# First heads chosen one by one, scores inside the next block, GLA output among the last input blocks, and both ends cut shorter, in a two-layer hybrid trunk

## What is computed

```python
hn = rms_norm(h, mix_norm[0]); h = h + gla_dilated_mixer(hn, ...)      # layer 0
hn = rms_norm(h, ffn_norm[0]); h = h + peer_ffn(hn, ...)
hn = rms_norm(h, mix_norm[1]); h = h + rglru_mixer(hn, ...)            # layer 1
hn = rms_norm(h, ffn_norm[1]); h = h + peer_ffn(hn, ...)
return rms_norm(h, final_norm)

# gla_dilated_mixer: gated linear attention (GLA, 4 heads) beside windowed attention (8 heads)
proj = h @ w_in
o_gla = gla_chunked(gq, gk, gv, log_a)
o_gla = o_gla * rsqrt(mean(o_gla * o_gla) + eps)                       # per head
o_gla = o_gla * head_gain * silu(gg)
return concatenate([o_gla, o_att]) @ w_out

# peer_ffn: 8 heads, 16 of 16,384 experts for each head and row
q = hf @ w_query;  s = q . sub_keys                                    # two halves of 128 keys
top_s, top_i = top_k(s, 16)                                            # of each half
best_s, best_c = top_k(all sums of a first and a second half, 16)      # ids = 128 * first + second
g = softmax(best_s)
out = sum over the 128 chosen of gelu(u[id] . x) * g * v[id]
```

## Time and profile before

| | us |
|---|---|
| median of 3 runs (lowest, highest) | 3009.1 (3007.6, 3010.1) |
| the profiled execution | 3012.2 |
| its span, first to last instruction | 3010.4 |
| busy in it: PE, DVE, ACT, POOL | 2663.3, 2155.2, 636.8, 992.6 |
| DMA over the span | 1,182.34 MB, mean 393 GB/s |

### The profile page before, as it was taken

One profiled execution on the slowest core, in us unless ns is written; L12 is line 12 of the kernel. 1 busy time (PEld: TensorE's weight loads), 2 busy tenths in 40 slices (PEclk: granted clock), 3 DMA queues, 4 the chain that ended last, 5 costly groups with the idle time before them and its releaser, 6 DMA issues.

```text
span 3010.4 us, 34985 instructions
## 1 busy us (share of the span) xinstructions
PE 2663.3 (88%) x11992; PEld 2185.1 (73%) x11992; DVE 2155.2 (72%) x6642; ACT 636.8 (21%) x1693; POOL 992.6 (33%) x1028
## 2 busy tenths in 40 slices
PE   8889999999999888989999898989999788877887
PEld 6778888767887676867887676868787566555555
DVE  1237867888578878677688777778678777678565
ACT  3221211163212216101111215201212110102001
POOL 0003333333323233333333333333333334333332
PEclk9899999999999999999999999999999999999999
DMA  5339999999999999999999999999999999999997
GB/s 181 103 133 421 419 424 409 426 381 402 411 398 387 402 426 414 414 427 426 426 407 419 414 427 418 407 426 424 427 415 392 409 426 424 427 425 411 427 426 330
DMA packets 166642, 1182.34 MB, mean 393 GB/s; under 512 B 19376, under 2 KB 19904, under 8 KB 23872
## 3 DMA queue, kind: packets, MB, share of 16 engines
q0 software_dynamic: 147456, 1073.81, 86.1%
q1 hardware_dynamic: 19008, 106.31, 9.0%
HBM read 1177.95 MB, written 2.10 MB: 392 GB/s over the span
## 4 chain that ended last, share of the span: by engine, by line
PE 52%; DMA 26%; DVE 12%; issue 8%; ACT 1%; POOL 0%; DVEq 0%; SPq 0%; ACTq 0%; POOLq 0%
PE main_bank L318 33%; DMA main_ring<-in_uv,main_idi 26%; PE main_bank L354 10%; PE main_bank L352 5%; DVE main_diagonal L301 2%; DVE main_ring L287 2%; DVE main_pick L199 1%; PE main_bank L522 1%; DVE main_pick L193 1%; DVE main_hid L287 1%; DVE main_topi L162 1%; DVE main_work L154 1%; DVE main_idf L206 1%; DVE main_topi L156 1%; PE main_bank L714 0%
## 5 line engine op out<-in xcount | busy, mean ns | idle before, releaser
L318 PE MATMUL main_bank<-main_ring,main_diagonal 128*128 128x256 f32 (+1 forms) x8160 | 1980.5, 389 | 301.4 <-DVE main_diagonal L301 300.3
L318 PEld LDWEIGHTS main_bank<-main_ring,main_diagonal 128*128 128x128 f32 x8160 | 1529.3, 192 | 660.0 <-DVE main_diagonal L301 440.7
L287 DVE CUSTOM_DVE_ANT_0 main_ring<-main_ring,main_bank 128x1024 f32<-128x1024 f32 x1024 | 1247.6, 1218 | 621.0 <-DMA main_ring<-in_uv,main_idi 609.7
L270 POOL DMA_INDIRECT main_ring<-in_uv,main_idi x1024 | 992.4, 969 | 1994.0 <-PE main_bank L318 1740.1
L292 ACT ACTIVATE main_act_out<-main_hid 128x1 f32<-128x1 f32 x1024 | 206.2, 203 | 2156.1 <-DVE main_hid L287 2154.9
L301 DVE TENSOR_SCALAR main_diagonal<-main_ident,main_act_out,main_gate 128x128 f32<-128x128 f32 x1024 | 358.8, 350 | 23.0 <-ACT main_act_out L292 14.0
L354 PE MATMUL main_bank<-main_xT,main_w_block 128*128 128x256 f32 x1408 | 359.3, 382 | 1.8 <-ACT main_xT L387 1.8
L354 PEld LDWEIGHTS main_bank<-main_xT,main_w_block 128*128 128x128 f32 x1408 | 269.1, 192 | 39.2 <-ACT main_xT L387 2.2
L354 PE MATMUL main_bank<-main_xT_query,main_w_block 128*128 128x256 f32 x512 | 124.9, 381 | 0.9 <-ACT main_xT_query L387 0.9
L354 PEld LDWEIGHTS main_bank<-main_xT_query,main_w_block 128*128 128x128 f32 x512 | 97.3, 191 | 15.1 <-ACT main_xT_query L387 1.2
L292 ACT ACT_TABLE_LOAD x82 | 105.2, 1283 | 1.4
(11 more groups left out here) (187 smaller groups left out, 1209.8 us busy)
## 6 DMA issues: line engine op xcount, KB each, us to landing
main_w_block<-in_w_query SPq DMA_DIRECT2D x32, 1024.0 KB, 9.4
main_w_block<-in_w_ab SPq DMA_DIRECT2D x24, 1024.0 KB, 8.0
main_ring<-in_uv,main_idi POOLq DMA_INDIRECT x1024, 10.7
main_w_block<-in_w_c_in SPq DMA_DIRECT2D x16, 1024.0 KB, 9.3
main_w_block<-in_w_out SPq DMA_DIRECT2D x8, 1024.0 KB, 6.9
main_w_block<-in_w_c_out SPq DMA_DIRECT2D x8, 1024.0 KB, 9.1
main_att_bias<-in_att_bias SPq DMA_DIRECT2D x16, 256.0 KB, 5.2
main_resid<-in_x SPq DMA_DIRECT2D x2, 1024.0 KB, 7.5
```

Of the source, the lines that this page charges most:

```text
L270: nc.gpsimd.indirect_dma_start(self.ring[n % self.bufs], None, self.uv[p // NT], bass.IndirectOffsetOnAxis(self.choice.idi[:, p % 2, k:k + ...
L287: self.nc.vector.tensor_tensor_reduce(out=row, in0=row, in1=self.ps[:, 6:8], scale=1.0, scalar=0.0, op0=ALU.mult, op1=ALU.add, accum_out=s ...
L318: last = self.nc.tensor.matmul(self.ps[:, 4 + at // T, at % T:at % T + wide], self.diagonal[:, n % DIAGS], self.ring[n % self.bufs][:, D + ...
```

## The change

1. Start: x is loaded as two tiles with a semaphore each, and the squares of a tile wait for it alone; ident and gains are waited for later. A Sqrt of a constant stands first on ScalarE.
2. GLA, first half: the two output tiles follow input pieces 169 and 174 (PE), 172 and 178 (ACT). The sigmoid of the gate goes in two halves of 256 columns, the first after piece 186, and now waits for GLA's squares, since its tile is moved onto theirs. The scale and head gain are applied to the output ahead of the gate, the gate in two halves. The turn of the mixed rows does the attention half first and waits for GLA in between. The second half of the rows uses the same functions in the ring, at k = 86 to 94.
3. Query: scores of head i-1 stand after the fourth piece of block i. ScalarE's exponential comes after all four query copies.
4. Choice: heads 0 and 1 are ranked and chosen one at a time; a semaphore `first` releases the first 16 gathers. Head 2's ranking moves into the ring at k = 5.
5. End: the last add, squares, scaling and store go in two halves of 512 columns; a Sqrt of a constant stands before the last squares.

```diff
-    def candidates(self, dve, g):
+    def candidates(self, dve, g, ks=range(2)):
...
+        nc, n, of = self.nc, len(ks), slice(ks[0], ks[-1] + 1)
...
-        nc.vector.tensor_copy(self.idi[:, p % 2, slots], self.idf[:]).then_inc(self.chosen, 1)
+        copied = nc.vector.tensor_copy(self.idi[:, p % 2, slots], self.idf[:, ks[0] * PK:(ks[-1] + 1) * PK])
+        if ks[-1] == 0:
+            copied.then_inc(self.first, 1)
+            return
+        copied.then_inc(self.chosen, 1)
...
-                if k % (2 * PK) == 0:
+                if n == 0:
+                    pool.wait_ge(self.choice.first, 1)
+                elif n == PK or k % (2 * PK) == 0:
                     pool.wait_ge(self.choice.chosen, p * self.choice.PAIRS + k // (2 * PK) + 1)
...
+    def add_halves(self, dve):
+
+        dve.wait_ge(self.half_done, 1)
+        for a in range(2):
+            if a:
+                dve.wait_ge(self.v_done, 2 * NT * HK)
+            half = self.resid[:, NT - 1, a * T:(a + 1) * T]
+            self.nc.vector.tensor_tensor(half, self.ps[:, 4 + a], half, ALU.add).then_inc(self.half_added, 1)
...
-        self.sg = own("gla_sg", 1024, [P, 2, GV_W])
+        self.sg = own("gla_sg", 2048, [P, 2, GV_W])
...
-        pe.wait_ge(self.gla_done, g + 1)
-        for d in range(KD):
+        for d in (4, 5, 6, 7, 0, 1, 2, 3):
+            if d == 0:
+                pe.wait_ge(self.gla_done, g + 1)
...
-    def gla_silu_act(self, act, g):
-        act.wait_ge(self.dec_there, g + 1)
-        act.wait_ge(self.w.taken, self.until(g, 11))
-        self.nc.scalar.activation(self.sg[g][:], self.gg[:], ACT.Sigmoid).then_inc(self.silu, 1)
+    def gla_silu_act(self, act, g, c):
+
+        act.wait_ge(self.ssd, g + 1)
+        act.wait_ge(self.w.taken, self.until(g, 10 + c))
+        cols = slice(c * BC, (c + 1) * BC)
+        self.nc.scalar.activation(self.sg[g][:, :, cols], self.gg[:, :, cols], ACT.Sigmoid).then_inc(self.silu, 1)
...
+    def gla_gated_dve(self, dve, g, c):
+
+        dve.wait_ge(self.silu, 2 * g + c + 1)
+        cols = slice(c * BC, (c + 1) * BC)
+        o, sg = self.mixed[g][:, :, cols], self.sg[g][:, :, cols]
+        self.link(dve, self.nc.vector.tensor_tensor(sg, sg, self.gg[:, :, cols], ALU.mult))
+        last = self.nc.vector.tensor_tensor(o, o, sg, ALU.mult)
+        if c:
+            last.then_inc(self.gla_done, 1)
...
+    def sqrt_act(self, act):
+
+        act.wait_ge(self.one_there, 1)
+        self.nc.scalar.activation(self.one[:, 1:2], self.one[:, 0:1], ACT.Sqrt)
...
-            sp.dma_start(resid[:, 0:2], x[:, 0:2]).then_inc(loaded[0], 16)
+            for t in range(2):
+                sp.dma_start(resid[:, t], x[:, t]).then_inc(x_in[t], 16)
...
-            act.wait_ge(loaded[0], 48)
+            final.sqrt_act(act)
             for t in range(2):
+                act.wait_ge(x_in[t], 16)
                 norms.squares(act, 0, mix0.rows[0], t)
             norms.root_mean(act, 0)
             norms.rows_scaled(act, 0, mix0.rows[0])
+            act.wait_ge(loaded[0], 32)
...
+                if n in (172, 178):
+                    mix0.gla_out_act(act, 0, n // 178)
+                if n == 186:
+                    mix0.gla_root_act(act, 0)
+                    mix0.gla_silu_act(act, 0, 0)
...
                 tail0.act_q(act, 0, i)
-                if i:
-                    tail0.act_scores(act, 0, i - 1)
-                if i == 2:
-                    choice.exponentials(act, 0, 0)
+                if i < 3:
+                    tail0.act_scores(act, 0, i)
+            choice.exponentials(act, 0, 0)
             norms.gains_in(act, 2, mix0.xT)
...
-            final.squares_act(act, NT - 1)
+            final.sqrt_act(act)
+            final.last_squares_act(act)
             final.root_act(act, NT - 1)
...
-            for i in range(3):
+            for i in range(2):
                 tail0.rank_dve(dve, 0, i)
-                if i == 1:
-                    choice.candidates(dve, 0)
-                    choice.greatest(dve, 0)
-                    choice.places(dve)
-                    choice.picked(dve)
-                    choice.numbers(dve, 0, 0)
+                choice.candidates(dve, 0, (i,))
+                choice.greatest(dve, 0, (i,))
+                choice.places(dve, (i,))
+                choice.picked(dve, (i,))
+                choice.numbers(dve, 0, 0, (i,))
...
-                        if k in (9, 17, 25, 33, 41):
+                        if k in (5, 9, 17, 25, 33, 41):
                             tail0.rank_dve(dve, 0, k // 8 + 2)
...
-            for t in range(2):
-                mix0.gla_out_pe(pe, 0, t)
+                if n in (169, 174):
+                    mix0.gla_out_pe(pe, 0, n // 174)
...
-            for i in range(4):
-                tail0.pe_query(pe, 0, i)
+            for x in range(4 * weights.PIECES):
+                tail0.pe_query_piece(pe, 0, x, 3)
```

More of the change, by code:

```diff
@@ L136, in __init__ @@
         self.links = 0
[L137 to L138 removed]
+        self.chain, self.diff, self.exped, self.first, self.chosen, self.gated = (
+            s.sem(f"choice_{x}") for x in ("chain", "diff", "exped", "first", "chosen", "gated"))
     def link(self, dve, ins):
@@ L319, in sum_rows @@
                                          self.ring[n % self.bufs][:, D + at:D + at + wide], start=k == 0, stop=k == HK - 1 and at % T + wide == T)
+            if n == 2 * NT * HK - 1 and at + wide == T:
+                last.then_inc(self.half_done, 1)
         last.then_inc(self.v_done, 1)
@@ new lines, in start_dve, with last_squares_act @@
+    def start_dve(self, dve):
+        self.nc.vector.memset(self.one[:, 0:1], 1.0).then_inc(self.one_there, 1)
+    def sqrt_act(self, act):
+        act.wait_ge(self.one_there, 1)
+        self.nc.scalar.activation(self.one[:, 1:2], self.one[:, 0:1], ACT.Sqrt)
+    def last_squares_act(self, act):
+        for a in range(2):
+            act.wait_ge(self.experts.half_added, a + 1)
+            cols = slice(a * T, (a + 1) * T)
+            self.nc.scalar.activation(self.rows[:, NT - 1, cols], self.resid[:, NT - 1, cols], ACT.Square, scale=float(D) ** -0.5,
+                                      accum_out=self.halves[:, a:a + 1]).then_inc(self.squared, 1)
@@ new lines, in last_mean_dve, with last_dve @@
+    def last_mean_dve(self, dve):
+        dve.wait_ge(self.squared, NT + 1)
+        self.nc.vector.scalar_tensor_tensor(self.ms[:, NT - 1:NT], self.halves[:, 0:1], EPS, self.halves[:, 1:2], ALU.add,
+                                            ALU.add).then_inc(self.mean, 1)
+    def last_dve(self, dve):
+        nc, c = self.nc, NT - 1
+        dve.wait_ge(self.rooted, NT)
+        nc.vector.reciprocal(self.rs[:, c:c + 1], self.root[:, c:c + 1]).then_inc(self.scaled, 1)
+        dve.wait_ge(self.scaled, NT)
+        for a in range(2):
+            cols = slice(a * T, (a + 1) * T)
+            nc.vector.scalar_tensor_tensor(self.rows[:, c, cols], self.resid[:, c, cols], self.rs[:, c:c + 1], self.gain[:, cols], ALU.mult,
+                                           ALU.mult).then_inc(self.there, 1)
```

102 lines of the change are left out of this document (49 added, 53 removed).

## The result

Median **2991.9 us** (2989.3 to 2992.9, 4 runs) against 3009.6 for the kernel before beside it (3007.6 to 3014.2, 4 runs): ratio 0.9938, 95% interval [0.992, 0.9955]. The interval leaves out 1, so the kernel is faster, by 17.7 us in this pair, where 25.5 was forecast; 2991.9 lies 1.4 us above the range. In four later sessions the changed kernel came out as here and the kernel before slower: over all sessions the kernel before takes 3014.2 us in the mean (84 runs), the changed kernel 2991.3 (19 runs). That is a gain of **22.9 us**.

A forecast was written before the change was run, and what follows sets the result against it. PE paces the input blocks, then PE and DMA the gathers; gains lie outside that ring. Start 2.6, GLA output 8.7, clock 2.1, first sum 9.6 and end 2.5 sum to 25.5: 3009.1 to 2983.6 us, range 2978.5 to about 2990.5.

The forecast's parts named there:

- the ring: Gathers of expert rows through 7 buffers, from PE's first expert sum: some 2,770 us that the change hardly enters.
- the clock: At the output projection: its first 64 records would no longer start at the lower PE clock, 2.1 us saved, bounds 0 to 2.1.
- Start: Kernel start: x in halves and the Sqrt table loaded early bring the first transpose 2.6 us forward, bounds 1.1 to 3.1.
- GLA output: Between input blocks and output projection: output tiles made among the last input pieces, projection 8.7 us earlier, bounds 6.5 to 9.5.
- first two heads: Query to first expert sum: earlier scores, heads chosen singly, exponential later; first sum 9.6 us earlier, bounds 8 to 11.6.
- end: After the last expert sum: add, squares, scaling and store in halves, Sqrt loaded early; 2.5 us saved, bounds 1.4 to 3.0.
- Does the ring start with PE: PE is full from the first expert sum, so everything after it shifts by 23.0 us; by the gathers' side 24.6.
- rival 1: Gathers carry the shift into later passes: 1.6 us more, 2.0 with a warm first sum; 2980.0 to 2982.0, chance 0.20.
- rival 2: PE's clock falls around GLA's output: 2.1 us lost, up to 3.1 more; 2985.7 to 2988.8 us, chance 0.20.
- The base, and the range: Span differences taken off the 3009.1 us median; range about 2978.5 to 2990.5, with 1.5 us for run differences at the low end.
- My own test for being wrong: Sum wrong if the first expert sum moves 23 us and the last does not, or 2,770 us between them changes by over 2.
- The slower rival (emptier ring): Buffers come back too late for the DMA queues, passes 3.7% longer: 74 us over 1,980 us, 3057 us, chance 0.02.

The follow-up runs named there:

- the fill: Changed kernel plus 14 unused identity transposes in PE's wait for GLA's gate and 4 ahead of the output projection: medians 2987.9 and 2989.4 us.

## Why the prediction was right and wrong

Two steps failed. The sum booked 2.1 us for the clock as a sure gain, and it took the rest of the kernel, base and ring, as known to 1.5 us. The parts that were added up from rows of waits held.

The first sum, in the mean of the profiles of the whole kernels (two before, four after):

```
                                            forecast   measured
start, to the first product                     2.6       2.4
first input block                               0         1.1
second input block to projection (GLA)          8.7       8.4
clock on the projection                         2.1      -0.85
first query block to first sum                  9.6       9.9
together                                       23.0      20.95
```

- **Start (2.6), GLA output (8.7), first two heads (9.6), end (2.5): right.** Measured in the first pair 2.39, 8.9 (149.41 - 138.13 - 2.39, of which 0.2 is the first input block), 9.6 and 2.45. (The start's two terms add up to 2.7, not 2.6; the second square begins 1.3 us earlier, not 1.6.) The added Sqrt load and SP's extra issue cost no more than was said: the first query block begins 169.27 - 138.13 = 31.1 us behind the projection (before 33.3, less the 2.1 of the clock), and the wait ahead of the first sum is the ACT chain alone. What the third head's move costs inside the ring is below what its scatter lets one see. Choosing one head took 9.6 us (180.42 to 190.01), forecast 9.7.
- **"Does the ring start with PE": right.** PE is at 199.12 of 199.80 us from the first sum on, and rival 1, the gathers' side, got nothing: the ring is not shorter.
- **The clock (2.1): this step failed.** I took two numbers of one profile, 16.20 and 14.08, for a price that the place always pays and that the change takes away. What the clock costs the projection is a toss in both kernels: 0.8 us before in the mean of five profiles, 2.2 after in the mean of seven, so the change loses some 1.4 us where I booked 2.1 as won. That the first pair showed the 2.1 us to the digit was luck, one profile of seven. Over the whole-kernel profiles the term was 3.0 us off, and the first input block, booked at nothing, gave 1.1 back (a toss as well, and perhaps partly the new start): 229.6 - 208.7 = 20.9 us, not 23.0. The reading that transposes hold the clock up was right, as the fill shows, though the rise at 225 us that I gave for it came in one profile of four; that waits of 1.9 and 0.9 us (measured 2.02 and 0.74) would not let it fall was wrong. This is rival 2's mechanism, given 0.20, and it should have been the likelier case, since in the profile of before PE had slowed behind a wait of just 0.85 us.
- **The base, and the range: this step failed too, and is the larger part of the miss.** Working in differences of one execution and taking them off a median of three runs (3009.1) was the plan; but the ring of one program varied by 5.5 us between four executions, and the kernel before takes 3014.2 in the mean. I allowed 1.5 us for it, at the low end of the range only, although the four times at hand (3007.6 to 3012.2) were already 4.6 apart. From 2983.6 to 2991.3 are 7.7 us: 5.1 of base, 2.1 of clock and first block, 0.5 of ring and tail, which is within the uncertainty. A range with 3 us of run scatter at both ends (the deviation of single runs is 3.2) would have held it.
- **My own test for being wrong misled.** I had written that a ring changed by over 2 us would refute the sum. It changed by 6.2 in the first pair and by 0.5, give or take 1, in the mean: one pair of profiles can't decide 2 us out of 2,770.
- The slower rival (emptier ring) did not come: 402 and 417 GB/s for 403 and 418.

**Open:** why the ring varies. The extra of the first pair is spread over passes of both signs (differences by 128 steps, in us: -0.6, +2.6, +2.8, -1.7, +2.9, -3.0, +0.4, +2.7). Over the 16 profiles its length goes weakly with the time that the clock spent at the lower level inside it (54.6 to 103.9 us; correlation 0.44, which 16 unrelated pairs reach in about one case of twelve): 60.0 us went with 2771.7 and 88.5 with 2777.8, but 103.9 with 2773.8. No run here separates cause from chance.

## What to carry to other kernels

Ahead of this long ring, which one engine paces at its start, what was taken from the chain to its first step was kept: 22.9 us by the runs, 23.4 by the rows of first sum and tail. The terms that were waits could be added up from rows to a few tenths. A gain that rests on the granted clock is a chance, not a duration: read several profiles, and where PE's waits can't be removed, try to fill them with transposes (here some 2.4 us of 2991). And take as the base of a forecast, and as its uncertainty, what many runs of the kernel show: the part that nothing touches was here the largest source of error.

## What the runs showed of the hardware

In the last 80 steps or so, where gathers pace the ring at one dot product per 2.4 us, every 32nd gather lands 1.0 us late, three times, in both kernels and at the same spacing (steps 952, 984, 1016 before; 944, 976, 1008 after). DVE's timeline of the changed kernel, the second row 3.42 us after the first instead of 2.4:

```profile
2781.12 1.22 DVE L297 CUSTOM_DVE_ANT_0 main_ring<-main_ring,main_bank 128x1024 f32<-128x1024 f32 x1 [0.92 <-DMA main_ring<-in_uv,main_idi]
...
2784.54 1.22 DVE L297 CUSTOM_DVE_ANT_0 main_ring<-main_ring,main_bank 128x1024 f32<-128x1024 f32 x1 [1.94 <-DMA main_ring<-in_uv,main_idi]
```

In the DMA view of 2781 to 2784 us one packet of 8 KB of the queue marked "instruction" stands among the gathers' packets; the same holds at the two later late gathers, and at all three of the kernel before, each time 2.2 us ahead of the late dot product:

```profile
q0 software_dynamic: 171, 1.27, 101.2%
q14 instruction: 1, 0.01, 0.6%
```

That the packet causes the delay is a reading, not tested, and not every such packet goes with one: the packet at 2810.1 us of the kernel before has no late gather behind it until 2821.0. From one late place to the next, 32 steps, the kernels agree to 0.02 us (79.34 and 79.32 before, 79.33 and 79.32 after).
